# First SwiGLU's up projection with seven quarter products for eight, sums of its weights formed in two chains of DMAs

## The chip, the cores and the metric

The kernel runs on one core of a Trainium2 chip. The time is device microseconds of that core for one execution; lower is better. All data are float32.

## The reference

The reference is two transformer blocks over 512 tokens of width 1024. The first block has a Fourier mixer, a gated recurrence and a feed-forward layer with a depthwise convolution. The second block has two layers: retention and a SwiGLU, then a short convolution and another SwiGLU. Every layer is modulated by six vectors (shift, scale, gate, twice) that come from a product of a condition vector with the adaptive weights `ada_w`. Cut to what matters here:

```python
def swiglu(h, w1, w3, w2):
    return (jax.nn.silu(h @ w1) * (h @ w3)) @ w2

for i in range(2):
    sh1, sc1, g1, sh2, sc2, g2 = ada_params(c, ada_w[i], ada_b[i])
    ax = rms_norm(hx, norm_mix[i]) * (1 + sc1) + sh1
    hx = hx + g1 * (retention_mixer(ax, ...) if i == 0 else conv_mixer(ax, ...))
    fx = rms_norm(hx, norm_ffn[i]) * (1 + sc2) + sh2
    hx = hx + g2 * swiglu(fx, ffn_w1[i], ffn_w3[i], ffn_w2[i])
```

Here h is 512 x 1024, w1 and w3 are 1024 x 2816 and w2 is 2816 x 1024.

## The kernel before, in words

**Layout and stream of weights.** Activations lie transposed, channels on partitions and 512 tokens in the free dimension. All weights come as one stream of 377 blocks of 128 x 1024 floats (512 KB). SP loads a block into one of two raw buffers (`w_raw`); ScalarE rounds it to `w_hi` (`split_hi`, L435, the copy is L444), and VectorE forms `w_lo` as the rest (`split_lo`, L446, L452). There are four buffers of each, so the split of a block waits for the end of the block four back, and beside the work on block b the split of block b+3 is made. Each product is three matmuls: hi x hi, hi x lo, lo x hi (`three`, L487, its matmul is L493). SP loads block n when `lo_ready` shows that block n-2 is split. A block is 24 matmuls of 128x128 weights with 512 columns.

**Stages and block numbers.** Retention is blocks 122 to 185 (`B_RET`), four heads of 16 blocks. The first SwiGLU's up projection is blocks 186 to 229 (22 pairs of tiles, one of w1 and one of w3), its down projection 230 to 251 (`B_SD0`), the convolution's input 252 to 275 (`B_CIN`), its output 276 to 283, and the second SwiGLU's up projection starts at 284 (`B_SW1`). Between two stages stands a transition: the norm over channels is formed in two halves of 256 tokens, and the first tiles of the next stage run between (`transition_act`, L614; `transition_dve`, L676).

**The first SwiGLU** (`swiglu_pe` L1289, `swiglu_act` L1783, `swiglu_dve` L2310) is a loop over pairs of tiles: PE makes the w1 tile in a bank of `bx` and the w3 tile in a bank of `by`, ScalarE applies silu (L1799), VectorE multiplies, ScalarE and VectorE split the hidden tile into `hid_hi` and `hid_lo`. Beside each block ScalarE loads one row of adaptive weights (128 x 1024, `ada_load` L455) into one of two buffers `ada_raw`, and VectorE reduces it against the condition vector (`ada_reduce` L463; L474, then a short add L485). Rows 81 to 124 are loaded here; four rows are reduced in the down projection (`down_dve` L2388, `down_act` L1827), which updates the residual `res` after each of eight output tiles.

**The second SwiGLU** makes four pairs of tiles (`TILEWISE`) in the same way, and 18 pairs (`N_QUADS`) with seven quarter products for eight. For one pair the weights form a 2 x 2 matrix (w1 or w3, even or odd tiles of the contraction) and the activations too (even or odd tiles, first or second 256 tokens); seven products of four contraction tiles by 256 columns, of sums of weights and of activations, take the place of eight (`quad_pe` L980, matmul L1015). One pair takes 3.5 blocks of weights, 84 matmuls with 256 columns. VectorE forms four combinations of the activations beside the first four pairs (`sums_dve` L934, `combined_hi` L947, `combined_lo` L964), and VectorE and ScalarE put the products together (`quad_first_act` to `quad_hidden_lo`). Here four raw buffers are used, `w_raw` and `ada_raw`.

**The sums of weights** (W22+W11 and so on) are formed in DRAM by GpSimd's DMAs (L3036 to L3054), five for each pair, in one chain: two copies (`quad_first`, L3047), one adding transfer of 512 KB (`quad_more`, L3050), two adding transfers of 256 KB within `quad_sums` (L3052, L3054). Each waits for the one before it (`summed`) and for a block that paces it. There are 18 x 5 of them over 78 blocks from block 124. SP waits for all of them, and for all 128 reduced rows, before the first block of the seven-product part.

Of the kernel before, what the change touches and what calls it, by code (L numbers as in the profile page):

```python
# [18 lines left out]
F32 = mybir.dt.float32  # L19
# [5 lines left out]
P = 128  # L25
# [31 lines left out]
B_SD0 = B_SW0 + 2 * HT  # L57
# [3 lines left out]
TILEWISE = 4  # L61
N_QUADS = HT - TILEWISE
B_QUAD = B_SW1 + 2 * TILEWISE
B_SD1 = B_QUAD + 7 * N_QUADS // 2
# [12 lines left out]


# [76 lines left out]
def program(nc, wstream, quad_first, quad_more, quad_sums, ada_kn, ada_nk, x_in, ctx1_in, ctx2_in, cols_in, crow_in, ident_in, masks_in,  # L155
            dft1_in, dft2_in, rope_in, dec_in, out):
    with ExitStack() as ctx:
# [26 lines left out]
        quad_raw = w_raw + ada_raw  # L184
# [34 lines left out]
        for n, at in ((1, r_arena + 72 * KB), (2, r_hx + 16 * KB)):  # L219
# [59 lines left out]
                for s in range(2)]  # L279
# [3 lines left out]
        t_norm = sb("t_norm", [P, KT, L], F32, r_hc + 52 * KB)  # L283
        t_raw = sb("t_raw", [P, 4, KT // 2, L // 2], F32, r_hc + 68 * KB)
        t_at = [(r_hc + 88 * KB, r_hc + 92 * KB), (r_crow, r_crow + 4 * KB), None, (r_crow + 8 * KB, r_scr + 8 * KB)]
        t_hi, t_lo = ([None if at is None else sb(f"t{n}_{h}", [P, KT // 2, L // 2], F32R, at[h == "lo"])
                       for n, at in enumerate(t_at)] for h in ("hi", "lo"))
# [107 lines left out]
        summed = sem("summed")  # L395
# [31 lines left out]
        def raw_at(b):  # L427

            if b.at < B_QUAD:
                return w_raw[b.at % RAW], raw_ready[b.at % RAW], b.loads()  # L430
            n, s = divmod(b.at - B_QUAD, 4)
            return (quad_raw[s], *((raw_ready[s], 16 * (B_QUAD // RAW + n + 1)) if s < RAW else
                                   (ada_in[s - RAW], 16 * (128 // 2 + n + 1))))
# [29 lines left out]
        def ada_reduce(dve, a, row, i=None, per=0, row_c=None):  # L463

            landed = 16 * (a // 2 + 1)
            dve.wait_ge(ada_in[a % 2], landed if i is None else i * (16 * per // 2) + landed)
            n = a if i is None else i * per + a
            w = ada_raw[a % 2]
# [142 lines left out]
        def normalised(nm, j):  # L611
            return t_norm[:, j, :] if nm is nffn1 else tnorm[j % 2][:]
# [217 lines left out]
        COMBINED = [0, 1, 3, 2]  # L830
# [6 lines left out]
        JX["cin"] = JX["sw0"] + HT  # L837
# [4 lines left out]
        JY["sd0"] = JY["sw0"] + HT  # L842
# [68 lines left out]

        def place(g, n):

            return divmod(7 * g + n, 2)

        def made(engine, g, form):

            b, second = place(g, PRODUCTS[g % 2].index(form))
            if second:
                engine.wait_ge(block_done, B_QUAD + b + 1)  # L920
            else:
                engine.wait_ge(q_form, OPENED + b + 1)
# [5 lines left out]
        def combined(n, lo=False):  # L928

            if t_hi[n] is None:  # L930
# [2268 lines left out]
```

## Time and profile before

| | us |
|---|---|
| median of 3 runs (2257.71 to 2259.14) | 2259.04 |
| the profiled execution's own time | 2258.87 |
| its span | 2257.1 |
| PE busy | 2239.3 |
| DVE busy | 1483.9 |
| ACT busy | 868.9 |
| POOL busy | 232.3 |

PE is TensorE's matmuls, PEld its weight loads, DVE is VectorE, ACT ScalarE, POOL GpSimd, SP SyncE; a q behind a name is that engine's queue of DMA issues. Busy times overlap. A matmul's own duration in the trace overlaps with the next one's, so its price is the distance of two starts. A wait row says who waited, for whom, how long in total, how often and how long at most. Times in a view are counted from the start of the span. The 326 MB that the DMA engines move are 144 GB/s in the mean.

### The profile page before, as it was taken

What the parts mean: (1) busy time and instruction counts of PE and PEld (TensorE: products, weight loads), DVE (VectorE), ACT (ScalarE), POOL (GpSimd) and SP (SyncE); (2) the same over time, 40 slices, a digit from 0 to 9 for tenths busy, and PEclk for the clock granted to TensorE, in tenths of its full rate; (3) what the DMA queues carried; (4) which work ended last, traced back from release to release, by engine and by line L of the source; (5) the groups of instructions that cost most, each with busy time, mean ns of one, the idle gap of its engine ahead of it and who ended that gap; (6) DMA issues with size and microseconds to landing.
All of it is one profiled execution on the core that took longest, in us unless ns stands there. A gap on an engine that the chain in (4) does not pass through costs nothing.

```text
span 2257.1 us, 31951 instructions
## 1 busy us (share of the span) xinstructions
PE 2239.3 (99%) x11632; PEld 1906.4 (84%) x11632; DVE 1483.9 (66%) x2287; ACT 868.9 (38%) x1248; POOL 232.3 (10%) x187
## 2 busy tenths in 40 slices
PE   9999999999999999999999999999999999999998
PEld 4888888888888898888888878888889889999987
DVE  5558766689999866755746467665436446777622
ACT  4534442355554343313233244323224223554422
POOL 0000000036674001011110100100000000000000
PEclk9999999999999999999999999999999999999999
DMA  8442115423324628475765657876432332555421
GB/s 316 159 131 74 58 61 186 149 66 103 101 93 148 221 71 236 116 191 146 181 170 139 177 132 221 254 232 195 149 103 72 106 101 68 177 183 182 159 94 56
DMA packets 90939, 326.10 MB, mean 144 GB/s; under 512 B 10064, under 2 KB 10960, under 8 KB 89680
## 3 DMA queue, kind: packets, MB, share of 16 engines
q1 hardware_dynamic: 58432, 213.90, 28.5%
q10 hardware_dynamic: 19440, 72.96, 9.9%
q0 software_dynamic: 12960, 37.75, 8.4%
q8 instruction: 74, 1.21, 0.2%
q14 instruction: 33, 0.27, 0.0%
HBM read 322.48 MB, written 39.85 MB: 161 GB/s over the span
## 4 chain that ended last, share of the span: by engine, by line
PE 94%; DVE 3%; issue 1%; DMA 1%; ACT 1%; SPq 0%; DVEq 0%
PE bank L493 81%; PE bank L1015 8%; PE bank L1490 1%; DMA res<-in_x 1%; DVE rstd L680 1%; DVE hx_lo L692 0%; PE bank L1572 0%; PE bank L1348 0%; DMA w_raw<-in_wstream 0%; PE bank L1545 0%; DVE w_lo L452 0%; ACT hx_hi L627 0%; DVE tnorm L686 0%; PE bank L1514 0%; ACT w_hi L444 0%
## 5 line engine op out<-in xcount | busy, mean ns | idle before, releaser
L493 PE MATMUL bank<-hx_hi,w_hi 128*128 128x512 f32 (+1 forms) x1648 | 622.1, 377 | 5.3 <-DVE hx_lo L692 4.6
L493 PE MATMUL bank<-hx_hi,w_lo 128*128 128x512 f32 (+1 forms) x1648 | 611.6, 371 | 0.0
L493 PE MATMUL bank<-hx_lo,w_hi 128*128 128x512 f32 (+1 forms) x1648 | 611.6, 371 | 0.0
L452 DVE TENSOR_TENSOR w_lo<-w_raw,w_hi 128x1024 fp32r<-128x1024 f32 x290 | 354.7, 1224 | 343.5 <-ACT w_hi L444 339.7
L444 ACT ACTIVATE w_hi<-w_raw 128x1024 fp32r<-128x1024 f32 x335 | 353.8, 1056 | 426.5 <-PE bank L493 305.6
L493 PEld LDWEIGHTS bank<-hx_hi,w_hi 128*128 128x128 f32 x1648 | 311.2, 189 | 61.7 <-issue 4.9
L493 PEld LDWEIGHTS bank<-hx_hi,w_lo 128*128 128x128 f32 x1648 | 311.1, 189 | 53.2
L493 PEld LDWEIGHTS bank<-hx_lo,w_hi 128*128 128x128 f32 x1648 | 311.3, 189 | 52.8 <-issue 1.4
L2681 DVE SCALAR_TENSOR_TENSOR bank<-zpad,cols,bank 128x512 f32<-128x512 f32 x352 | 232.1, 773 | 4.6 <-ACT bank L2081 4.6
L493 PE MATMUL bank<-hid_hi,w_hi 128*128 128x512 f32 (+1 forms) x594 | 218.5, 368 | 0.0
L493 PE MATMUL bank<-hid_hi,w_lo 128*128 128x512 f32 (+1 forms) x594 | 217.2, 366 | 0.0
L493 PE MATMUL bank<-hid_lo,w_hi 128*128 128x512 f32 (+1 forms) x594 | 217.1, 366 | 0.0
L474 DVE CUSTOM_DVE_ANT_0 ada_raw<-ada_raw,crow 128x1024 f32<-128x1024 f32 x128 | 157.2, 1228 | 1.2 <-DMA ada_raw<-in_ada_nk 1.0
L493 PEld LDWEIGHTS bank<-hid_hi,w_lo 128*128 128x128 f32 x594 | 112.0, 189 | 18.2
L493 PEld LDWEIGHTS bank<-hid_hi,w_hi 128*128 128x128 f32 x594 | 112.0, 189 | 18.1
L493 PEld LDWEIGHTS bank<-hid_lo,w_hi 128*128 128x128 f32 x594 | 112.1, 189 | 17.8
L3005 POOL TENSOR_TENSOR w_lo<-w_raw,w_hi 128x1024 fp32r<-128x1024 f32 x44 | 105.2, 2408 | 5.6 <-ACT w_hi L444 5.5
L452 DVE TENSOR_TENSOR w_lo<-ada_raw,w_hi 128x1024 fp32r<-128x1024 f32 x42 | 51.5, 1225 | 53.9 <-ACT w_hi L444 53.9
L1015 PE MATMUL bank<-hx_hi,w_hi 128*128 128x256 f32 x288 | 81.6, 283 | 0.0
L1015 PE MATMUL bank<-hx_lo,w_hi 128*128 128x256 f32 x288 | 81.5, 283 | 0.0
L1015 PE MATMUL bank<-hx_hi,w_lo 128*128 128x256 f32 x288 | 81.5, 283 | 0.0
L444 ACT ACTIVATE w_hi<-ada_raw 128x1024 fp32r<-128x1024 f32 x42 | 44.5, 1060 | 67.3 <-PE bank L1015 43.9
(368 smaller groups left out, 3595.7 us busy)
## 6 DMA issues: line engine op xcount, KB each, us to landing
w_raw<-in_wstream SPq DMA_DIRECT2D x316, 512.0 KB, 3.5
ada_raw<-in_ada_nk ACTq DMA_DIRECT2D x128, 512.0 KB, 4.3
quad_sums<-in_quad_first POOLq DMA_DIRECT2D x36, 512.0 KB, 5.2
ada_raw<-in_wstream SPq DMA_DIRECT2D x25, 512.0 KB, 3.4
w_raw<-quad_sums SPq DMA_DIRECT2D x19, 512.0 KB, 3.8
quad_sums<-in_quad_more POOLq DMA_DIRECT2D x18, 512.0 KB, 7.6
quad_sums<-quad_sums POOLq DMA_DIRECT2D x36, 256.0 KB, 5.6
ada_raw<-quad_sums SPq DMA_DIRECT2D x17, 512.0 KB, 4.0
```

The source lines that it names most:

```text
L444: nc.scalar.activation(w_hi[nb.at % RING][:], src[:], ACT.Copy).then_inc(hi_ready, 1)
L452: nc.vector.tensor_tensor(w_lo[nb.at % RING][:], raw_at(nb)[0][:], w_hi[nb.at % RING][:].bitcast(F32), ALU.subtract).then_inc(lo_ready, 1)
L474: nc.vector.tensor_tensor_reduce(w[:], w[:], crow[:, row, :], 1.0, 0.0, ALU.mult, ALU.add, ada_sum[:, a % 4:a % 4 + 1]).then_inc(ada_done, 1)
L493: ins = nc.tensor.matmul(out_ap, s, m, start=first and at == 0, stop=last and at == n - 1)
L680: nc.vector.reciprocal(nm.rstd[:, HALF[h]], nm.std[:, HALF[h]]).then_inc(nm.rec, 1)
L1015: ins = nc.tensor.matmul(dst[:, HALF[half]], w[:, cut], mx, start=opens and j == 0 and m == 0, stop=j == KT // 2 - 1 and m == 2, skip_grou ...
L1490: ins = nc.tensor.matmul(dst, level_k[c % 2][:, h * P:(h + 1) * P], pair_halves(hq, c, r - 1, h), start=True, stop=True)
L2681: nc.vector.scalar_tensor_tensor(out=grid, in0=zpad[s][k][:, t // 3:t // 3 + ROWS, t % 3:t % 3 + GRID], scalar=cols[:, bass.ds(cw, 1)], in ...
L3005: nc.gpsimd.tensor_tensor(w_lo[nb.at % RING][:], w_raw[nb.at % RAW][:], w_hi[nb.at % RING][:].bitcast(F32), ALU.subtract).then_inc(lo_read ...
```

## The change

The first SwiGLU's up projection gets the form that the second has: four pairs tile by tile, 18 pairs with seven products. All functions of the form take the index w of the SwiGLU (0 or 1), and their code is used for both. With it:

- The stream is numbered anew: the first seven-product part is blocks 194 to 256, `B_SD0` is 257, `B_CIN` 279, `B_SW1` 311, the second seven-product part starts at 319, and there are 404 blocks. What SP loads and where to stands in a table (`loads`); SP's loop ends before block 194, and the rest of its list is written out.
- 36 pairs of weights need sums. Two chains run side by side, taken in turn: 24 pairs over blocks 124 to 180, 12 pairs over blocks 258 to 303.
- Rows 81 to 127 of the adaptive weights move: the reduction of row 80 stands in the first four pairs, rows 81 to 111 beside the first down projection, rows 112 to 127 beside the convolution's input, two to each group of three blocks. They use four buffers, `ada_raw` and two in the region of `crow`.
- The normalised activations of the first SwiGLU stay in a buffer of their own (`t_norm[0]`).

```diff
@@ constants
+QUAD_BLOCKS = 7 * N_QUADS // 2
+B_QUAD = [B_SW0 + 2 * TILEWISE]
+B_SD0 = B_QUAD[0] + QUAD_BLOCKS
...
+ADA_BEFORE = 81
+EARLY_SUMS = 24
...
@@ buffers
-        t_norm = sb("t_norm", [P, KT, L], F32, r_hc + 52 * KB)
+        t_norm = [sb(f"t_norm{w}", [P, KT, L], F32, r_hc + (16, 52)[w] * KB) for w in range(2)]
...
+        ada_more = [sb(f"ada_raw{s}", [P, D], F32, r_crow + 4 * KB * (s - 1)) for s in (2, 3)]
...
@@ loads
+        for n in range(N_BLOCKS):
+            for w in range(2):
+                if B_QUAD[w] <= n < (B_SD0, N_BLOCKS)[w]:
+                    loads[n] = landing(("raw0", "raw1", "ada0", "ada1")[(n - B_QUAD[w]) % 4], n)
+            if n not in loads:
+                loads[n] = landing("raw%d" % ((n if n < B_SD0 else n - B_SD0) % 2), n)
+            if n == B_SD0:
+                row_loads = {a: landing(("ada1", "ada0", "ada2", "ada3")[(a - ADA_BEFORE) % 4], None) for a in range(ADA_BEFORE, 128)}
...
@@ ada_load
+            if i is None and a >= ADA_BEFORE:
+                if a >= ADA_BEFORE + 4:
+                    act.wait_ge(ada_done, a - 3)
+                act.dma_start(row_loads[a][0][:], ada_nk[a]).then_inc(row_loads[a][1], 16)
+                return
...
@@ where rows and sums stand
-        SUMS = 5 * N_QUADS
-        SUMS_FROM, SUMS_OVER = B_RET + 2, (B_SW1 - B_RET - 6) // 2
+        ADA_ROWS = [range(ADA_BEFORE + (3 * n) // 2, ADA_BEFORE + (3 * n + 3) // 2) for n in range(HT - 1)]
+        CIN_ROWS = [range(112 + 2 * u, 114 + 2 * u) for u in range(KT)]
+        SUMS_IN = [(0, EARLY_SUMS, B_RET + 2, B_SW0 - 6), (EARLY_SUMS, 2 * N_QUADS, B_SD0 + 1, B_SW1 - 8)]
...
@@ SP
+            for w in range(2):
+                plain = B_QUAD[w] - w * 2 * N_QUADS
+                sp.wait_ge(ada_done, (ADA_BEFORE, 128)[w])
+                for c in range(2):
+                    sp.wait_ge(summed[c], 16 * 5 * (w + 1) * N_QUADS // 2)
+                for n in range(B_QUAD[w], (B_QUAD[1], N_BLOCKS)[w]):
+                    slot, landed, _, previous = loads[n]
+                    if previous is not None:
+                        sp.wait_ge(lo_ready, previous + 1)
...
+                    sp.dma_start(slot[:], src).then_inc(landed, 16)
...
@@ PE
-            swiglu_pe(pe, B_SW0, JX["sw0"], JY["sw0"], nffn0)
-            hidden_down_pe(pe, B_SD0, JY["sd0"], sw_l[0], 0, nmix1, none)
+            def quads_pe(w):
+                for g in range(N_QUADS):
+                    quad_pe(pe, w, g)
+                pe.wait_ge(q_post, OPENED + 4 * (N_QUADS * w + N_QUADS - 1))
...
+            swiglu_pe(pe, B_SW0, JX["sw0"], JY["sw0"], nffn0, TILEWISE)
+            quads_pe(0)
+            hidden_down_pe(pe, B_SD0, JY["sd0"], sw_l[0], 0, nmix1, lambda ct: quads_out(0) if ct == 0 else None)
...
@@ ScalarE
-            swiglu_act(act, 0, B_SW0, JX["sw0"], JY["sw0"], 80)
-            down_act(act, B_SD0, JY["sd0"], [(nmix1, None)], lambda n: ada_load(act, 125 + n) if n < 3 else None, none)
...
+            quads_act(0)
+
+            def rows_act(n):
+                if n == 0:
+                    act.wait_ge(block_done, B_SD0)
+                    act.wait_ge(lo_ready, B_SD0)
+                for a in [*(ADA_ROWS[0] if n == 0 else ()), *(ADA_ROWS[n + 1] if n + 1 < len(ADA_ROWS) else CIN_ROWS[0])]:
+                    ada_load(act, a)
+
+            down_act(act, B_SD0, JY["sd0"], [(nmix1, None)], rows_act, none)
...
@@ ScalarE, in the convolution's input, after the second tile of a group
+                    for a in (CIN_ROWS[4 * i + u + 1] if 4 * i + u + 1 < KT else ()):
+                        ada_load(act, a)
...
@@ VectorE
-            swiglu_dve(dve, 0, B_SW0, JY["sw0"], 80)
-            modulation(88, COLS["mix"] + 8, 8)
-            down_dve(dve, B_SD0, JY["sd0"], lambda j: ada[:, 72 + j:73 + j], (nmix1,),
-                     lambda n: ada_reduce(dve, 124 + n, ROW_C2) if n < 4 else None)
-            dve.wait_ge(ada_cols, 128)
+            quads_dve(0)
+
+            def rows_dve(n):
+                for a in (ADA_ROWS[n] if n < len(ADA_ROWS) else ()):
+                    ada_reduce(dve, a, ROW_C2)
+                if n < len(ADA_ROWS) and 95 in ADA_ROWS[n]:
+                    dve.wait_ge(ada_cols, 96)
+                    modulation(88, COLS["mix"] + 8, 8)
+
+            down_dve(dve, B_SD0, JY["sd0"], lambda j: ada[:, 72 + j:73 + j], (nmix1,), rows_dve)
+            dve.wait_ge(ada_cols, 112)
...
@@ VectorE, in the convolution's input, after each of the first two splits of a group
+                        if kind < 2:
+                            ada_reduce(dve, CIN_ROWS[4 * i + u][kind], ROW_C2)
...
@@ GpSimd
+            def summing(first, last, since, until):
+                for q in range(first, last, 2):
+                    for step in range(5):
+                        for c in range(2):
+                            at = 10 * ((q - first) // 2) + 2 * step + c
+                            pool.wait_ge(block_done, since + at * (until - since) // (5 * (last - first)))
+                            if q or step:
+                                pool.wait_ge(summed[c], 16 * (5 * (q // 2) + step))
...
+            for part in SUMS_IN:
+                summing(*part)
```

## Rows read from the trace of the kernel before

**Rows 1.** The page: its span, and the first line of its part 1.
```profile
span 2257.1 us, 31951 instructions
...
PE 2239.3 (99%) x11632; PEld 1906.4 (84%) x11632; DVE 1483.9 (66%) x2287; ACT 868.9 (38%) x1248; POOL 232.3 (10%) x187
```

**Rows 2.** Chain that ended last, 1943 to 2125 us: start us, us, what.
```profile
1943.03 5.75 PE bank L1015 x48
1948.77 0.04 issue
1948.81 175.91 PE bank L1015 x1464
```

**Rows 3.** Timeline of ACT, 1562 to 1592 us: start us, us, engine, line, operation.
```profile
1563.60 1.04 ACT L444 ACTIVATE w_hi<-w_raw 128x1024 fp32r<-128x1024 f32 x1
...
1574.48 1.04 ACT L444 ACTIVATE w_hi<-w_raw 128x1024 fp32r<-128x1024 f32 x1
```

**Rows 4.** Busy by stage: length, PE, PEld, DVE, ACT, POOL, clock, DMA, GB/s.
```profile
824.00:970.00 146.00, 146.00 (x767) 125.29 (x768) 110.85 (x168) 54.50 (x84) 12.80 (x18) 1.00 0.58 160
1358.00:1480.00 122.00, 122.00 (x613) 104.23 (x613) 82.89 (x133) 41.09 (x56) 10.71 (x15) 1.00 0.80 244
1600.00:1700.00 100.00, 100.00 (x445) 82.90 (x444) 33.40 (x38) 23.27 (x25) 0.00 (x0) 1.00 0.35 110
...
1943.00:2125.00 182.00, 181.96 (x1515) 181.73 (x1514) 136.00 (x191) 92.57 (x138) 0.00 (x0) 1.00 0.56 184
```

**Rows 5.** DMA queues and issues, 1358 to 1480 us; last: us to landing.
```profile
q10 hardware_dynamic: 3306, 12.05, 29.3%
q1 hardware_dynamic: 3260, 11.85, 28.2%
q0 software_dynamic: 2044, 5.82, 22.5%
...
quad_sums<-in_quad_first POOLq DMA_DIRECT2D x6, 512.0 KB, 6.3
quad_sums<-quad_sums POOLq DMA_DIRECT2D x6, 256.0 KB, 7.4
quad_sums<-in_quad_more POOLq DMA_DIRECT2D x3, 512.0 KB, 9.3
```

**Rows 6.** Timeline of POOL, the first eleven issues of sums.
```profile
845.51 0.70 POOL L3047 DMA_DIRECT2D quad_sums<-in_quad_first  x1 [127.89 <-PE bank L493]
...
911.33 0.54 POOL L3047 DMA_DIRECT2D quad_sums<-in_quad_first  x1 [5.55 <-DMA quad_sums<-quad_sums]
```

**Rows 7.** Instructions of L474 on DVE, 1358 to 1620 us.
```profile
L474 DVE CUSTOM_DVE_ANT_0 ada_raw<-ada_raw,crow x48: 1217/1219/1226, 1370.1 to 1613.4; 128x1024 f32<-128x1024 f32 x48
L474 DVE DVE_READ_ACCUMULATOR2_ANT ada_sum<- x48: 81/83/88, 1371.3 to 1614.5; 128x1 f32 x48
```

**Rows 8.** Timeline of ACT, 1386 to 1392 us.
```profile
1390.23 1.06 ACT L444 ACTIVATE w_hi<-w_raw 128x1024 fp32r<-128x1024 f32 x1 [0.86 <-DMA w_raw<-in_wstream]
```

**Rows 9.** Waits of PE: who waited for whom, us in total, times, longest us.
```profile
PE bank L493 <- DVE res L2722: 1.7, 5, 0.6
```

**Rows 10.** Instructions of L1146, all: duration ns, first and last start us.
```profile
L1146 SPq DMA_DIRECT2D w_raw<-in_wstream x24: 327/332/338, 1926.1 to 2205.3; - x24
```

**Rows 11.** Waits of DVE, 1358 to 1620 us.
```profile
DVE ada_raw L474 <- DMA ada_raw<-in_ada_nk: 0.7, 1, 0.7
```

**Rows 12.** Chain that ended last, 1320 to 1340 us.
```profile
1325.34 7.74 DMA w_raw<-in_wstream
...
1336.22 3.91 PE bank L493 x16
```

**Rows 13.** Busy time, clock and DMA share of three short windows.
```profile
1348.00:1351.00 3.00, 0.56 (x5) 0.35 (x3) 2.71 (x4) 1.49 (x3) 0.53 (x1) 1.00 0.44 123
1351.00:1354.00 3.00, 2.78 (x16) 2.52 (x17) 2.96 (x7) 0.56 (x2) 0.83 (x1) 0.76 0.16 60
1354.00:1358.00 4.00, 4.00 (x25) 3.94 (x25) 3.89 (x10) 3.50 (x7) 0.00 (x0) 0.75 0.94 174
```

More of the change, by code:

```diff
@@ L394, in program, with landing @@
         t_sum, t_hi_ready, t_lo_ready, t_shifted = opened[6:10]
-        summed = sem("summed")
+        ada_in_more = opened[10:12]
+        summed = [sem(f"summed{c}") for c in range(2)]
+        loads = {}
+        counts = {"ada0": (ADA_BEFORE + 1) // 2, "ada1": ADA_BEFORE // 2, "ada2": 1, "ada3": 1}
+        slots = {"raw0": (w_raw[0], raw_ready[0]), "raw1": (w_raw[1], raw_ready[1]), "ada0": (ada_raw[0], ada_in[0]),
+                 "ada1": (ada_raw[1], ada_in[1]), "ada2": (ada_more[0], ada_in_more[0]), "ada3": (ada_more[1], ada_in_more[1])}
+        last_in = {}
+        def landing(name, n):
+            counts[name] = counts.get(name, 0) + 1
+            before_it, last_in[name] = last_in.get(name), n
+            return (*slots[name], 16 * counts[name], before_it)
+        for n in range(N_BLOCKS):
[6 more added lines that the diff above has]
+                row_loads = {a: landing(("ada1", "ada0", "ada2", "ada3")[(a - ADA_BEFORE) % 4], None) for a in range(ADA_BEFORE, 128)}
         class Norm:
@@ L1013, in quad_pe @@
                     xh, xl = x(j)
-                    for m, (w, mx) in enumerate(((w_hi[slot], xh), (w_hi[slot], xl), (w_lo[slot], xh))):
-                        ins = nc.tensor.matmul(dst[:, HALF[half]], w[:, cut], mx, start=opens and j == 0 and m == 0,
+                    for m, (form_w, mx) in enumerate(((w_hi[slot], xh), (w_hi[slot], xl), (w_lo[slot], xh))):
+                        ins = nc.tensor.matmul(dst[:, HALF[half]], form_w[:, cut], mx, start=opens and j == 0 and m == 0,
                                                stop=j == KT // 2 - 1 and m == 2, skip_group_check=True)
@@ L1127, in _ @@
                 crow_load(row, crow_landed)
-            with sp.Fori(1, B_QUAD // RAW - 1) as i:
+            with sp.Fori(1, B_QUAD[0] // RAW - 1) as i:
                 for s in range(RAW):
@@ L2904, in _, with quads_dve, combinations @@
             dve.wait_ge(nffn0.lo, nffn0.tiles + 2 * KT)
[L2905 to L2909 removed]
+            def quads_dve(w):
+                made_sums = sums_dve(dve, w)
+                def combinations(u):
+                    if w == 0 and u == 0:
+                        ada_reduce(dve, ADA_BEFORE - 1, ROW_C2)
+                    if 1 <= u < 4:
+                        next(made_sums)
+                        if u == 2:
+                            next(made_sums)
+                            combined_lo(dve, w, 0, 1)
+                        elif u == 3:
+                            combined_lo(dve, w, 1, 2)
+                            combined_lo(dve, w, 3, 3)
+                swiglu_dve(dve, w, (B_SW0, B_SW1)[w], JY["sw0" if w == 0 else "sw1"], None, TILEWISE, combinations)
+                for u in range(TILEWISE, 4):
+                    combinations(u)
+                for g in range(N_QUADS):
+                    at = list(windows(g))
+                    split_lo(dve, Block(B_QUAD[w] + at[0]))
+                    if g == 0:
+                        combined_lo(dve, w, 2, 4)
+                    else:
+                        quad_hidden_dve(dve, w, g - 1)
+                    split_lo(dve, Block(B_QUAD[w] + at[1]))
+                    if g >= 1:
+                        quad_hidden_lo(dve, w, g - 1)
+                    quad_mid_dve(dve, w, g)
+                    split_lo(dve, Block(B_QUAD[w] + at[2]))
+                    quad_inner_dve(dve, w, g)
+                    for b in at[3:]:
+                        split_lo(dve, Block(B_QUAD[w] + b))
+                    quad_outer_dve(dve, w, g)
+                quad_hidden_dve(dve, w, N_QUADS - 1)
+                quad_hidden_lo(dve, w, N_QUADS - 1)
```

339 lines of the change are left out of this document (154 added, 185 removed).

## The prediction

> **What bounds the kernel now.** I read the page first: PE is busy for 2239.3 of 2257.1 us [rows 1]. PE is the bound in nearly every stage, so a change counts by the PE time it removes and by the waits it puts in front of PE. Second the chain that ended last, over the second SwiGLU, where the seven-product form runs already: 48 and 1464 matmuls of 256 columns from 1943.03 to 2124.72 (1948.81 plus 175.91), with 0.04 us of issue between them [rows 2]. This is the price of what the first SwiGLU is to get. Third ScalarE's timeline in the first SwiGLU, for the price of what goes: a split of a block starts when the block four before it is done, so equal splits are one tile pair apart [rows 3]. Fourth the busy time by stage [rows 4], because the change moves transfers and VectorE work between stages. Fifth the DMA queues where weights, adaptive rows and sums already run together [rows 5], and the sums' own pace on GpSimd [rows 6].
>
> **The products.** A pair of tiles of the first SwiGLU takes 10.88 us (1574.48 less 1563.60) [rows 3]: 48 matmuls of 512 columns, 226.7 ns each. A pair by seven products is 84 matmuls of 256 columns; 18 pairs take 181.69 us together, 10.09 us a pair, 120.2 ns a matmul [rows 2]. Half the columns cost more than half the time (113.3 ns), so an eighth less work gives 7.2%. Eighteen pairs: 18 x 10.88 = 195.8 us go, 181.7 come: **-14.1 us**.
>
> The Trainium skill (TensorE: Matmul & The Clock Gate, Back-to-back issue gap) gives an isolated gap of N/2.4 + 2.5 ns, so 215.8 and 109.2 ns. By that the sum would be 18 x (48 x 0.2158 - 84 x 0.1092) = 21.3 us saved, an estimate. The trace measures 226.7 and 120.2 ns for these very forms, so the measured 14.1 stays.
>
> **The work around them.** Forming the four combinations of activations, the opening of the banks and the last wait before the down projection are copies of what the second SwiGLU does. There DVE is busy for 136 of 182 us, ACT for 92.6, and PE for 181.96 of 182 [rows 4]; what hides them is PE's own time. VectorE has one thing more in the opening four tiles, the reduction of row 80 (1.22 us and some 0.3 us of small instructions) [rows 7]; in the first SwiGLU before, VectorE makes such a reduction beside every block, and PE still has 122.00 of 122 us [rows 4]. If that cover were gone it would cost 1.5 us once. I take 0.
>
> **SP's queue.** From block 194 on SP runs an unrolled list. It first waits for 81 reduced rows and for 45 transfers of each chain of sums; behind that wait stand all later weight loads. The row is reduced at the start of the SwiGLU, before SP could issue this load anyway, whose buffer comes free later. For the second SwiGLU it waits for row 128 (reduced in the convolution) and the last sums. In time both cost 0; late, they are rival 2.
>
> **Sums in retention.** Before, one chain makes 18 tiles, paced over 78 blocks; afterwards two chains make 24 tiles over 56 blocks. GpSimd issues them and has nothing else there. An unpaced step takes 6.6 us (845.51 to 911.33, ten steps) [rows 6]. The plan: 64 blocks run between 824 and 1358 us [rows 4], 8.3 us each, so 60 steps of a chain in 467 us, 7.8 us a step. GpSimd takes the chains in turn, so both go at the pace of the slower. No row shows two chains. Below: 6.6 us a step, as alone. Above: 13.2, one chain's transfer wholly behind the other's. I take 9.5, nearer the first, since only a part of a step is transfer: three tiles of five steps take 22.5% of 122 us, 9.2 us a tile, 1.8 a step [rows 5]. The first 18 tiles then need 45 x 9.5 = 428 us and are ready at 1273, well before 1390.23, when block 194 was split before [rows 8]. The last six run on to 845 + 570 = 1415, beside the first products, whose share of DMA is 0.56 [rows 4]; two chains add 2 x 9.2/47.5 = 0.39. That fits. In retention they raise 0.58 [rows 4] by 0.39 less 9.2/33 = 0.28, to 0.7. Weight blocks land somewhat later, but are split two to three blocks ahead. I take 0; bounds -0.6 (the longest wait for res there goes) [rows 9] and +6 (rival 3).
>
> **Rows and sums beside the first down projection.** Rows 81 to 124 leave the SwiGLU. 31 rows (81 to 111) are loaded and reduced beside 21 of the 22 down blocks, where four were before, and 16 beside the convolution's input. VectorE per block of 5.44 us (24 of 226.7 ns): a split 1.2, 1.5 rows at 1.5, updates and squares 0.5, together 4.0 us; before it was busy for 33.4 of 100 us [rows 4, 7]. It fits. ScalarE only issues. For DMA I use the 122 us with all three kinds [rows 5]: 28.2% for 23 blocks is 1.50 us a block, 29.3% for 23 rows 1.55 us a row, and 9.2 us a tile of sums. In the down stage: blocks 1.50/5.44 = 0.28, rows 31 x 1.55/119.7 = 0.40, sums as planned 12 x 9.2/(45 x 5.44) = 0.45. Together **1.13, more than there is**. So something is late. If it is the sums, planned from 1600 over 245 us and needed about 1926, when SP issued the first loads of the second seven-product part before [rows 10], it costs nothing. If it is the rows, VectorE falls behind by up to 0.13 x 119.7 = 15.6 us by the end, of which 7 are covered, since the last row is due at step 20 of 22: +8. I take 0, because rows are issued a block ahead into four buffers, and at share 0.80 [rows 4] VectorE waited 0.7 us for rows in all [rows 11]. In the convolution: blocks 0.28, rows 16 x 1.55/131 = 0.19, sums 0.45: 0.92, which fits; its first reduction goes ahead of a split that waits for ScalarE anyway.
>
> **Sum.** Profiled execution 2258.87 us (span 2257.1 and 1.8 around it), 0.2 us below the median of the three runs, 2259.04. 2258.87 - 14.1 = **2244.8 us**. A measurement of this kernel can tell 0.2% (4.5 us) from no change.
>
> **Rivals.**
> 1. *The rows are what waits* in the overfull down stage, and VectorE is late for the transition. For it: 1.13, and two chains at once. Against: PE 122.00 of 122 at 0.80. Price up to +8: 2245 to 2253, say 2250. The Trainium skill (DMA: Bandwidth & Descriptors, Queues, rings and completion order) says that each engine goes round the queue rows packet by packet; both chains are on GpSimd's one queue, so by it the sums can't crowd out the other two, and the shortage falls on them. No row here shows a full stage.
> 2. *The chains of sums are too slow and SP stands still.* Place: SP's two waits. Block 194's load must go by about 1388, so 45 steps have 543 us: it decides from 12.1 us a step. The last 12 tiles, 30 steps, have from 1600 to about 1933: 11.1 us. Each us a step beyond costs 45 or 30 us, so from 11.6 us in the second part the gain is gone (0.5 x 30 = 15). At 13.2 both are late, by 594 - 543 = 51 and 396 - 333 = 63 us: 2359 us, **slower**. For it: with one chain under load the landings have medians of 6.3, 9.3 and 7.4 us [rows 5], 7.3 a step and with the issue above 8. Against: they would have to grow by half again.
> 3. *Weight blocks land late in retention.* The load at 1325.34 took 7.74 us with a sum in flight, and PE's matmul at 1336.22 hung on its split [rows 12]. If two chains make that 9.3, as the slowest kind of sum [rows 5], it is +1.6 at each of four heads: 2251. Against: the chain of waits shows this at one head only, and there PE was kept 0.6 us at most [rows 9].
> 4. *The clock.* PE was busy for only 0.56 of the 3 us from 1348; the granted clock was then 0.76 and 0.75 for 7 us, so for some 3.5 us at the level of 1.2 GHz: 0.24 x 3 + 0.25 x 4 = 1.7 us lost [rows 13]. If that goes, 2243.1.
>
> **How the numbers follow.** Forecast 0.70; rival 1 0.12, rival 2 0.04, rival 3 0.09, rival 4 0.05. Low end 2258.87 - 14.1 - 1.7 - 0.6 = 2242.5. High end 2251, with rival 3 and most of rival 1. Left out are rival 2 and the top of rival 1, together under 0.1. Faster by over 0.2% means below 2254.5: all but rival 2 and 0.02 for rivals 1 and 3 coming together: 0.94. Same 0.02, slower 0.04.
>
> **What would show it.** The first SwiGLU's 1512 seven-product matmuls take about 182 us with PE busy throughout, and no new wait stands before them. DMA share above 0.9 in the first down projection, the sums landing 8 us and more after issue and ending late; VectorE waiting for rows by some us, PE for none. ScalarE's waits for weights grow in retention without PE's. Wrong would be: PE waiting for w_lo at block 194 or in the second SwiGLU (rival 2), for res or w_lo in the down projection (rival 1), or a matmul spacing other than 120 ns.

## The result, and the profile after

| | before | after |
|---|---|---|
| median of 18 runs each, us | 2258.31 (2257.38 to 2259.63) | 2266.97 (2261.3 to 2276.02) |
| ratio | | 1.0039, 95% interval 1.0032 to 1.0046 |
| profiled execution's own time, us | 2258.87 | 2264.04 |

The change makes the kernel slower by 0.4%, where the prediction had it faster by 0.6%. The runs of after are also far more spread: 15 us from the fastest to the slowest, against 2.

I read the page first. Its lines for span, PE and the chain that ended last:

```profile
span 2262.2 us, 32938 instructions
...
PE 2230.9 (99%) x12280; PEld 1928.4 (85%) x12280; DVE 1559.0 (69%) x2419; ACT 908.5 (40%) x1321; POOL 295.2 (13%) x277
...
PE bank L530 60%; PE bank L1057 16%; DMA w_raw<-in_wstream 8%; DVE w_lo L480 2%; ACT w_hi L472 1%; PE bank L1536 1%; DMA ada_raw<-in_ada_nk 1%; DVE hx_lo L729 1%; DMA res<-in_x 1%; DVE rstd L717 1%; PE bank L1618 0%; PE bank L1394 0%; DVE cacc L3044 0%; PE bank L1591 0%; DVE rstd L2911 0%
```

PE is busy for 8.4 us less than before [rows 1], yet the span is longer. So PE now waits, and the chain says for what: DMA's loads of `w_raw` alone hold 8% of it, 180 us.

Next PE's waits (engine, line of the matmul, line of what it waited for: total, times, longest):

```profile
PE bank L530 <- DVE cy_lo L3052: 8.2, 1, 8.2
PE bank L530 <- DVE res L2786: 4.6, 5, 3.3
...
PE bank L530 <- DVE w_lo L480: 3.2, 6, 1.9
```

New are one wait of 8.2 us for `cy_lo` (the convolution's input), one of 3.3 us for `res` in retention, where the longest was 0.6 before [rows 9], and longer waits for splits (`w_lo`). Third the busy time by stage, with the granted clock, DMA's share and GB/s last in each line: retention, the seven-product part, the down projection, transition and convolution's input, then five short stretches around the two long waits.

```profile
845.00:1313.00 468.00, 464.03 (x2127) 385.58 (x2126) 281.19 (x402) 142.21 (x199) 84.92 (x120) 0.99 0.85 214
1404.00:1586.00 182.00, 181.96 (x1515) 181.75 (x1514) 135.76 (x190) 92.55 (x138) 0.00 (x0) 1.00 0.57 178
1586.00:1705.00 119.00, 118.71 (x574) 100.06 (x574) 79.22 (x136) 29.83 (x35) 17.09 (x25) 1.00 1.01 329
1727.00:1850.00 123.00, 119.87 (x526) 97.78 (x525) 75.18 (x113) 34.40 (x45) 21.18 (x30) 1.00 0.92 255
1103.00:1106.00 3.00, 0.59 (x1) 0.50 (x2) 2.62 (x4) 1.79 (x3) 1.28 (x2) 0.77 0.75 92
1106.00:1109.00 3.00, 3.00 (x9) 2.32 (x8) 1.75 (x3) 0.00 (x0) 0.76 (x1) 0.50 0.77 200
1109.00:1113.00 4.00, 4.00 (x14) 3.21 (x13) 0.75 (x1) 0.00 (x0) 0.62 (x2) 0.70 0.96 248
1855.00:1859.00 4.00, 0.00 (x0) 0.00 (x0) 3.09 (x6) 1.11 (x2) 0.00 (x0) 0.57 0.43 131
1859.00:1863.00 4.00, 3.64 (x10) 2.94 (x11) 3.16 (x5) 2.04 (x3) 0.00 (x0) 0.58 0.29 69
```

The seven-product part is as forecast: 181.96 us of PE in 182, as in the second SwiGLU [rows 4]. The down projection, with DMA full (1.01), costs PE 0.3 us. The losses are in the two stretches where DMA's share is 0.85 and 0.92. And after each long wait PE runs slower for a while: after PE had been busy for 0.59 of 3 us the granted clock was 0.50 of full speed (that is 1.2 GHz) with PE busy throughout the next 3 us, and after the wait for `cy_lo` (0.00 us of 4) it was 0.57 and 0.58 for two stretches of 4 us. At the first that is 3 x 0.46 + 3 + 4 x 0.6 = 6.8 us at the lower level, at the second 4 x 0.86 + 4 x 0.84 = 6.8 us; in the first PE still stood for some 0.8 us of the 6.8, so it costs some 3.0 us, and in the second for more than half, so it costs some 1.5.

What delays the transfers shows in the median time from issue to landing, here for the weight blocks in the transition and the convolution's input, where the copies of the sums took 7.8:

```profile
w_raw<-in_wstream SPq DMA_DIRECT2D x22, 512.0 KB, 8.2
```

The chain around the wait for `cy_lo` (start, us, what) shows how a late block reaches PE:

```profile
1809.34 8.59 DMA w_raw<-in_wstream
...
1817.94 1.07 ACT w_hi L472
...
1820.18 0.69 DVE cpad L3035
...
1824.26 1.05 ACT w_hi L472
...
1825.33 1.24 DVE w_lo L480
...
1826.59 10.74 DMA w_raw<-in_wstream
...
1845.99 6.10 DMA w_raw<-in_wstream
...
1852.12 1.06 ACT w_hi L472
...
1854.35 0.69 DVE cpad L3035
...
1857.88 0.64 ACT cy_hi L2341
...
1859.36 2.93 PE bank L530 x6
```

The chain returns to a load once in three blocks: 1809.34, 1826.59, 1845.99. In between stand the landing and 8.66 us of work that is made one after the other: ScalarE's `w_hi`, the multiply and the steps of `cacc` on VectorE (`cpad` to `cacc` L3048, 3.5 us), `cy_hi`, the next `w_hi`, the next `w_lo`, and only then does SP load into the raw buffer that this frees. PE's work in three blocks is 72 matmuls of 226.7 ns, 16.3 us. By this working the stage stands landings of 16.3 - 8.66 = 7.7 us, an estimate from one chain; at 8.59 and 10.74 us the turns took 17.25 and 19.40. Single later ones it stands as long as blocks are split ahead: of the 14.5 us lost behind block 190 (the table below) some 12 fell in the last group of the convolution. At the end VectorE, in order, waits for `w_hi` (1852.12) of a block that PE needs only later, with the `cacc` steps that PE needs now behind it.

The same in retention, once in this run:

```profile
1092.34 9.82 DMA w_raw<-in_wstream
...
1102.26 1.06 ACT w_hi L472
...
1103.35 0.05 DVE w_lo L480
...
1104.61 0.76 DVE res L2786
```

A load took 9.82 us; VectorE stood before the split of that block, and behind it the update of `res` that frees PE's bank.

### The profile page after: what moved, and what is told of

It reads as the page before. It is cut to its first block, busy times and chain, and to the rows that moved or that the text cites. A ratio compares the mean times of both kernels' runs of the same rounds, so it can differ in the third digit from the quotient of the medians.

```text
span 2262.2 us, 32938 instructions
## 1 busy us (share of the span) xinstructions
PE 2230.9 (99%) x12280; PEld 1928.4 (85%) x12280; DVE 1559.0 (69%) x2419; ACT 908.5 (40%) x1321; POOL 295.2 (13%) x277
## 4 chain that ended last, share of the span: by engine, by line
PE 80%; DMA 9%; DVE 6%; ACT 2%; issue 2%; SPq 0%; DVEq 0%; ACTq 0%
PE bank L530 60%; PE bank L1057 16%; DMA w_raw<-in_wstream 8%; DVE w_lo L480 2%; ACT w_hi L472 1%; PE bank L1536 1%; DMA ada_raw<-in_ada_nk 1%; DVE hx_lo L729 1%; DMA res<-in_x 1%; DVE rstd L717 1%; PE bank L1618 0%; PE bank L1394 0%; DVE cacc L3044 0%; PE bank L1591 0%; DVE rstd L2911 0%
## 5 line engine op out<-in xcount | busy, mean ns | idle before, releaser
L530 PE MATMUL bank<-hx_hi,w_hi 128*128 128x512 f32 (+1 forms) x1360 | 510.2, 375 | 7.4 <-DVE hx_lo L729 4.2
L530 PE MATMUL bank<-hx_lo,w_hi 128*128 128x512 f32 (+1 forms) x1360 | 499.7, 367 | 0.0
L530 PE MATMUL bank<-hx_hi,w_lo 128*128 128x512 f32 (+1 forms) x1360 | 499.6, 367 | 0.0
L530 PEld LDWEIGHTS bank<-hx_hi,w_hi 128*128 128x128 f32 x1360 | 257.2, 189 | 53.6 <-issue 7.8
L530 PEld LDWEIGHTS bank<-hx_hi,w_lo 128*128 128x128 f32 x1360 | 257.1, 189 | 42.4
L530 PEld LDWEIGHTS bank<-hx_lo,w_hi 128*128 128x128 f32 x1360 | 257.4, 189 | 41.0 <-issue 1.4
L1057 PE MATMUL bank<-hx_hi,w_hi 128*128 128x256 f32 x576 | 163.1, 283 | 0.1
L1057 PE MATMUL bank<-hx_hi,w_lo 128*128 128x256 f32 x576 | 163.0, 283 | 0.0
L1057 PE MATMUL bank<-hx_lo,w_hi 128*128 128x256 f32 x576 | 163.0, 283 | 0.0
L1057 PE MATMUL bank<-t_hi,w_hi 128*128 128x256 f32 x432 | 122.3, 283 | 0.0
```

What stands on the lines that cost most here:

```text
L530: ins = nc.tensor.matmul(out_ap, s, m, start=first and at == 0, stop=last and at == n - 1)
L1057: ins = nc.tensor.matmul(dst[:, HALF[half]], form_w[:, cut], mx, start=opens and j == 0 and m == 0, stop=j == KT // 2 - 1 and m == 2, skip ...
```

## The experiments

Eleven kernels ran. For a common measure the table gives, for one profiled execution of each, how much later the last matmul of a block ended than in the run without sums, with the difference at block 110 taken off (worked out from the traces' matmuls). So each column is a loss made in one stretch of one execution, and the medians need not follow it. The medians are over the runs of each.

| run | until block 120 | retention, to 190 | down projection to convolution's input, to 306 | median us |
|---|---|---|---|---|
| after | 0.0 | 6.1 | 14.5 | 2266.97 |
| e1_no_sums | 0 | 0 | 0 | 2244.24 |
| e2_no_late_sums | 0.0 | 9.7 | 0.0 | 2250.75 |
| e3_no_early_sums | 0.0 | -0.1 | 20.2 | 2259.84 |
| e4_no_row_loads | 0.0 | 0.3 | 0.0 | 2245.2 |
| e5_order | 0.0 | 0.0 | 13.3 | 2259.5 |
| f1_four_raw | 0.0 | 3.4 | 0.6 | 2246.36 |
| f2_sums_from_102 | 15.6 | 3.8 | 18.0 | 2280.4 |
| f3_all | 17.1 | 9.6 | 0.3 | 2265.05 |
| f5_all_30 | 13.7 | 3.2 | 0.0 | 2263.16 |
| g1_four_raw_res_first | 0.0 | 0.0 | 0.6 | 2243.63 |
| g2_all_orders | 0.0 | 0.2 | 0.0 | 2243.96 |

**e1_no_sums.** Are the sums the whole loss?

```diff
-                for c in range(2):
-                    sp.wait_ge(summed[c], 16 * 5 * (w + 1) * N_QUADS // 2)
...
-                        src = quad_sums[w * N_QUADS + 2 * q + half // 4, :, (half - 1) % 3 * BLK:((half - 1) % 3 + 1) * BLK]
+                        src = quad_first[w * N_QUADS + 2 * q + half // 4, :, (half - 1) % 3 * BLK:((half - 1) % 3 + 1) * BLK]
...
-            for part in SUMS_IN:
-                summing(*part)
```

> The changed kernel without any of the sums' transfers: SP reads the unsummed quad_first in place of quad_sums (same bytes, same pace) and waits for no sum. Left out: the sums of weights. Contention theory (the sums' transfers make weight blocks land late, the two raw buffers then pace PE, in-order VectorE is late): all the loss of 20 us goes, 2243 to 2247 us, spread of a few tenths as in the kernel before. Rival (the new form, the moved reductions on VectorE or SP's new waits cost it): 2260 us or more. Mixed: in between.

Measured: 2244.24 us (2243.88 to 2244.89), ratio 0.9938 (0.9925 to 0.995). That is the forecast of 2244.8 to 0.6 us, with the same products, rows and splits. All of the 22.7 us that after loses against it comes with the sums. The busy time of the transition and the convolution's input (the columns as above):

```profile
1727.00:1850.00 123.00, 122.69 (x541) 101.27 (x541) 80.99 (x118) 37.92 (x48) 0.00 (x0) 1.00 0.48 156
```

And the landing of its blocks in that stretch:

```profile
w_raw<-in_wstream SPq DMA_DIRECT2D x25, 512.0 KB, 3.6
```

PE works 122.69 of 123 us, DMA's share is 0.48, a block lands in 3.6 us.

**e2_no_late_sums** (the last 12 tiles are not formed) and **e3_no_early_sums** (the first 24 are not): do the two losses add?

```diff
-            for part in SUMS_IN:
+            for part in SUMS_IN[:1]:
```

```diff
-            for part in SUMS_IN:
+            for part in SUMS_IN[1:]:
```

> Only the second part of the sums is left out (12 tiles over blocks 258 to 303); the last 12 pairs read unsummed weights. Contention theory: what the profile shows lost in the convolution's input and behind it (about 11 us and more in slower runs) goes, the 5.5 us of retention stay: 2249 to 2253 us, spread smaller. Rival (the early sums in retention are the main cost): above 2258 us.

> The first 24 tiles' sums are left out (those blocks are read from the first quarter's forms, so the second factor's sums are missing there); the last 12 tiles are made as in the changed kernel, with its two raw buffers. Theory (the losses of the two stretches are separate and add): the retention is as before, the convolution's input loses what it lost in the changed kernel (cy_lo wait of 4 to 8 us with its half clock, 12 to 14 us in all), so 2244.2 + 12 to 16 = 2256 to 2260. Rival (the convolution loses because the retention has put the stages out of step): under 2252.

Measured: 2250.75 us (2247.47 to 2253.19) and 2259.84 us (2255.33 to 2270.36). Over the run without sums that is 6.5 us for the early sums and 15.6 for the late ones, together 22.1 of 22.7. The loss of the late sums comes without the early ones and the other way round, so they are separate. That the two medians add to within 0.6 us is partly luck: e4_no_row_loads and f1_four_raw below have the retention of e2_no_late_sums and lose 1.0 and 2.1 us in all over the run without sums, where this one lost 6.5. PE's waits in e3_no_early_sums:

```profile
PE bank L530 <- DVE cy_lo L3052: 5.7, 1, 5.7
PE bank L530 <- DVE w_lo L480: 4.8, 8, 2.8
...
PE bank L575 <- DVE std L555: 2.2, 1, 2.2
PE bank L530 <- DVE res L2786: 1.4, 4, 0.6
```

The wait for `cy_lo` is there, and `res` is back at 0.6. The wait for `std`, the norm's sum of squares, is at the end of the down projection: VectorE made it behind the split of a block that took 9.35 us to land and behind the reduction of one row. With the half clock after it that is 4.2 of the 20.2 us of the table; in after the same place lost 0.8. In e2_no_late_sums it is the other way:

```profile
PE bank L530 <- DVE res L2786: 6.3, 4, 3.4
```

**e4_no_row_loads.** Rows 81 to 127 are not loaded; their reductions stay on VectorE, with the condition row for both factors. All sums stay.

```diff
-                act.dma_start(row_loads[a][0][:], ada_nk[a]).then_inc(row_loads[a][1], 16)
```

> Rows 81 to 127 are not loaded; their reductions stay on VectorE, of the condition row with itself. Left out: those rows of the adaptive weights. All sums stay. Theory that both kinds of transfer must come together to be too much: the down projection falls from a DMA share of 1.0 to 0.6 and the convolution's input from 0.92 to 0.75, loads land near 6 us, the loss behind 1586 us goes, 2249 to 2254 us. Rival (the sums alone are enough): 2260 us or more.

Measured: 2245.2 us (2244.19 to 2251.65), ratio 0.9951 (0.9939 to 0.9964), 4 us under the range that I expected, since the retention lost less than 5. With the sums in place and DMA's share still 0.82 a block lands in 6.1 us in the convolution's input:

```profile
w_raw<-in_wstream SPq DMA_DIRECT2D x24, 512.0 KB, 6.1
```

6.1 + 8.66 = 14.8 us is under the 16.3 of three blocks, and the stretch loses nothing. So the sums alone don't make the late loss: it needs landings as late as rows and sums make together. That the retention lost nothing in this profile is chance: its code and its transfers are those of after, and so are e5_order's, with 0.0.

**e5_order.** In the convolution's last group the split of the block three ahead goes behind the `cy` steps, on ScalarE and VectorE.

```diff
-                        if i or u or kind:
+                        if (i or u or kind) and 3 * (4 * i + u) + kind < 23:
                             split_lo(dve, Block(B_CIN + 3 * u + kind, i, 12))
...
+            split_lo(dve, Block(B_COUT - 1))
             dve.wait_ge(ada_cols, 128)
```

> Everything as in the changed kernel, but in the last of the eight groups of the convolution's input ScalarE and VectorE do the split of the block three ahead after the convolution's own chain (cacc, cy_hi, cy_lo) and not before it. Theory (in-order engines: the chain PE needs stands behind a split that waits for a late block; the wait then halves PE's clock): the 8.2 us wait for cy_lo and the 3.4 us of low clock behind it shrink to the 0.3 us of before, 2256 to 2261 us. Rival (the wait only moves, since the same late block is missing next): no change beyond 2 us from 2267.

Measured: 2259.5 us (2255.35 to 2266.34, and one run of 6035.72 us; without it the median is 2258.41), ratio 1.0009 (1.0 to 1.0018), 7.5 us under after. PE's waits:

```profile
PE bank L530 <- DVE w_lo L480: 5.0, 11, 1.9
...
PE bank L530 <- DVE cy_lo L3054: 3.6, 1, 3.6
```

The wait for `cy_lo` is 3.6 us instead of 8.2, but PE waits 5.0 us for splits, 11 times: the order doesn't cure the stretch, and the loop of load, splits and `cacc` before it stays too slow. How much the order itself brings isn't shown: in the profiled executions the stretch lost 13.3 us instead of 14.5, and the rest of the difference is the retention, which has the same code in both.

**f1_four_raw.** The mechanism's own test: leave all traffic, and give the loads more time.

```diff
+        raw_more = [sb(f"raw_more{s}", [P, BLK], F32, r_hc + (88 + 4 * s) * KB) for s in range(2)]
...
+            if B_SD0 + 4 <= n < B_SW1:
+                loads[n] = landing(("raw2", "raw3", "raw0", "raw1")[(n - B_SD0) % 4], n)
...
+                    if n == B_SD0 + 4:
+                        sp.wait_ge(block_done, B_SD0)
```

> From block 261 on (second half of the first SwiGLU's down stage, the transition, the convolution's input) the weight blocks have four raw buffers instead of two; nothing else differs from the changed kernel. Theory (what costs the time behind the first SwiGLU is the latency of the block loads: with two buffers a pair of blocks comes every landing time + 2.4 us, so 8.2 us of landing is too much for 10.9 us of products): the waits for cy_lo go back from 8.2 us to under 1 us, the half clock at their side goes, the splits' margins before the products stay over 5 us, and the time is 2266.97 - 10 = about 2257, at most 2260; the retention's loss of about 5 us stays. Rival (the DMA engines' throughput itself is what lacks in that stretch: 92% are busy): blocks then queue deeper and land later still, and the time stays at 2264 to 2268.

Measured: 2246.36 us (2244.96 to 2248.15), ratio 0.9948 (0.9935 to 0.9961). The stretch of the convolution's input:

```profile
1727.00:1850.00 123.00, 122.69 (x542) 101.27 (x541) 80.83 (x119) 36.58 (x46) 20.54 (x29) 1.00 0.96 266
```

The landings there, of the two old raw buffers and of the two new ones:

```profile
w_raw<-in_wstream SPq DMA_DIRECT2D x12, 512.0 KB, 7.0
raw_more<-in_wstream SPq DMA_DIRECT2D x12, 512.0 KB, 7.5
```

DMA's share is higher than in after (0.96), the blocks land in 7.0 to 7.5 us, and PE works 122.69 of 123 us, as without any sums. The rival, that throughput is short, falls: the stage lacked buffers, not bandwidth. These medians are under the 7.7 us, so this run alone doesn't show that four buffers stand later landings; f3_all does. It has four buffers too (and the order of e5_order), and loses nothing here with a median of 8.0 in `w_raw` (7.2 in the other two):

```profile
1754.00:1877.00 123.00, 122.69 (x542) 101.27 (x541) 79.22 (x115) 38.16 (x48) 20.30 (x28) 1.00 0.93 257
...
w_raw<-in_wstream SPq DMA_DIRECT2D x12, 512.0 KB, 8.0
```

Nor is the median landing the measure for two buffers. f2_sums_from_102, with two, has 7.3 us in the same stretch (both are later than after here, by what they lost before), and PE stands still for 4.9 of 123 us:

```profile
1746.00:1869.00 123.00, 118.13 (x512) 95.09 (x510) 71.33 (x106) 32.90 (x43) 20.02 (x28) 1.00 0.92 252
...
w_raw<-in_wstream SPq DMA_DIRECT2D x21, 512.0 KB, 7.3
```

Its longest landing there is 13.2 us, after's 11.6, that of e4_no_row_loads, which loses nothing, 7.9. So single late blocks count, and the 7.7 us of the mean turn is no limit below which nothing is lost.

The time of f1_four_raw came out 10 us lower than I expected. Of the 20.6 us under after, 15.6 is what e3_no_early_sums showed for the late sums (I had expected 10); the rest would be the retention, which lost less in these runs than in those of e2_no_late_sums (2.1 us over the run without sums, against 6.5), with the same code there. Why, stays open.

**f2_sums_from_102.** A lower rate of sums in retention, by an earlier start.

```diff
-        SUMS_IN = [(0, EARLY_SUMS, B_RET + 2, B_SW0 - 6), (EARLY_SUMS, 2 * N_QUADS, B_SD0 + 1, B_SW1 - 8)]
+        SUMS_IN = [(0, EARLY_SUMS, B_DOWN + 2, B_SW0 - 6), (EARLY_SUMS, 2 * N_QUADS, B_SD0 + 1, B_SW1 - 8)]
```

> The first 24 tiles' sums are spread over blocks 102 to 180 instead of 124 to 180, a step of a tile each 10 us or so instead of 7.8; the last 12 tiles as in the changed kernel. Theory (in the retention the sums' rate sets the share of the DMA engines, 0.85, and with it the landing of the blocks, 6.4 us): the share there falls to about 0.78, the blocks land in about 5.6 us, no load of nearly 10 us falls beside a res update, and the time falls by 3 to 6 us to 2261 to 2264. Rival (the loss is made by any single late load, however rare, or by the stretch before 124 having no room either): no change, or a new wait before block 124; 2266 to 2270.

Measured: 2280.4 us (2277.31 to 2281.62), ratio 1.0095 (1.0081 to 1.011), worse than both. DMA's share from 845 to 1313 fell to 0.72, but the stretch before it, the last transition before retention, suffers. Its busy time, the granted clock third from the end:

```profile
770.00:800.00 30.00, 25.72 (x105) 20.82 (x104) 21.73 (x41) 10.45 (x17) 5.27 (x7) 0.89 0.94 253
800.00:845.00 45.00, 41.15 (x249) 36.49 (x248) 27.26 (x45) 17.21 (x27) 8.32 (x13) 0.92 0.90 216
```

The chain there (start, us, what):

```profile
767.26 9.30 DMA w_raw<-in_wstream
...
779.07 10.56 DMA w_raw<-in_wstream
...
790.62 0.70 ACT sq L546
...
792.49 0.44 DVE c_std L555
```

Loads took 9.30 and 10.56 us there, and the sums of squares and the `std` of the norm, which PE waits for (4.3 us for `c_std` and 3.5 for `std`, with the clock at 0.89 and 0.92), stood behind the splits. Neither of my numbers held; the rival named the place. The 3.8 us of its second column fall before block 150, next to this transition; from there to block 190 this execution lost nothing.

**f3_all** (four raw buffers, the early start, the order of e5_order) and **f5_all_30** (the same with 30 tiles early and 6 late):

```diff
-EARLY_SUMS = 24
+EARLY_SUMS = 30
```

> Both of the above (four raw buffers from block 261 on, the first 24 tiles' sums spread from block 102 on) and the order in the convolution's last group (the split of the block that is three ahead stands behind the last cy operations on ScalarE and VectorE). Theory: all of what the sums cost but the down stage's 0.9 us is back: 2245 to 2250, faster than before by 0.4 to 0.6%. Rival (throughput): the order alone brings what it did, 2257 to 2262.

> As the run of all three edits, with 30 of the 36 tiles of sums made early (blocks 102 to 180) and 6 late instead of 24 and 12. The first part's rate is then again about that of the changed kernel (a step each 8 us), the second's is halved. Theory (retention's loss comes from the rate): the retention loses its 5 us again and the late stages nothing, 2249 to 2253, slower than with 24 and 12. Rival (the late stages still lose more than the retention): 2244 to 2248, faster than with 24 and 12.

Measured: 2265.05 us (2261.88 to 2272.44) and 2263.16 us (2260.64 to 2265.29). Both miss, since both hold the early start, which costs 17.1 and 13.7 us before block 120. What they do show: behind the first SwiGLU both lose at most 0.3 us, and in f3_all some 6 of the 9.6 us of the second column were lost in the middle of retention (one wait of 4.0 us for `res`, and the half clock), although the rate of sums was lower and DMA's share only 0.72. So the loss there doesn't go by the rate alone.

**g1_four_raw_res_first** and **g2_all_orders.** If in retention it is the split ahead of the update that makes the loss, the order cures it at the full rate. The second adds the order of e5_order.

```diff
             def wo_dve(b0, jy, i, head0, split_from=0, nm=None, beside=none):
...
-                    if n >= split_from:
-                        split_lo(dve, b)
                     for u in range(2):
...
+                    if n >= split_from:
+                        split_lo(dve, b)
                     beside(n)
```

> As the run with four raw buffers, and in the retention's output projections VectorE makes both updates of the residual (which free TensorE's banks) before the split of the block three ahead, not behind it. Theory (the retention loses by a late load that holds VectorE ahead of an update): no wait for res over 1 us, no half clock in the retention, 2244 to 2245.5, 1 to 2 us under the run with four raw buffers alone (2246.4). Rival (the late loads hit the products themselves, or the later split makes the next load late): 2246 to 2250, with waits for w_lo in the retention.

> As the run before (four raw buffers, updates of the residual first), and the order of the convolution's last group (split behind the last cy operations). Theory: the buffers already cover the convolution's input, so the order adds at most the 0.6 us that stretch still loses: 2243.5 to 2245.5. Rival (the order costs once the buffers are there): over 2246.

Measured: 2243.63 us (2243.14 to 2245.74) and 2243.96 us (2243.44 to 2245.35), both with a ratio of 0.9938 (0.9925 to 0.9951). The first one's PE waits:

```profile
PE bank L535 <- DVE w_lo L485: 0.6, 4, 0.2
PE bank L535 <- DVE res L2791: 0.6, 1, 0.6
```

Its busy time in retention, and in the transition with the convolution's input:

```profile
845.00:1313.00 468.00, 467.57 (x2151) 388.36 (x2150) 285.50 (x403) 146.76 (x204) 84.83 (x120) 1.00 0.87 216
1727.00:1850.00 123.00, 122.69 (x541) 101.28 (x540) 79.36 (x115) 38.16 (x48) 20.06 (x28) 1.00 0.93 259
```

DMA's share is 0.87 and 0.93, as high as in after, a block in retention still lands in 6.6 us (6.4 in after), and PE works as without sums. Against f1_four_raw, the kernel that it differs from by the order alone, this is 2.7 us less. The ranges of two sets of five runs overlap there, but over g1 and g2 together the longest of ten runs is 2245.74, and over the three kernels that have the old order and no late loss (e2_no_late_sums, e4_no_row_loads, f1_four_raw) the fifteen runs go up to 2253.19. So the order takes the retention's losses away. The whole loss is gone, with every sum and row in place, and this version beats both kernels: faster than the kernel before by 0.6%. The order in the convolution adds nothing once the buffers are there.

## Why the prediction was wrong

**The products, -14.1 us: right.** The seven-product part took PE 181.96 us of 182, and the run without sums came to 2244.24 us against the forecast 2244.8. By the gap that the Trainium skill gives (TensorE: Matmul & The Clock Gate, Back-to-back issue gap) it would have been 2258.87 - 21.3 = 2237.6, an estimate; the measured spacing was the better price.

**The work around them, SP's queue: right.** No wait stood before the seven-product part, and SP waited for no sum. Rival 2 did not occur: the 60 steps of a chain began at 845.2 and the last at 1298.3 us, 7.7 us a step, the planned pace. I had taken 9.5; two chains hardly delayed each other. The share was mis-sized by this: I had 0.7 in retention, and it was 0.85. Two chains at 7.7 us a step take 0.54, with 10.5 us of all engines a tile (53.6% of 468 us for 24 tiles) where I had 9.2. And my 0.58 was from a stretch whose first 21 us had no sums; from 845 to 1313 it was 0.62 before.

**Rows and sums in the down projection: nearly right in the outcome.** The share was full, 1.01 at 329 GB/s, as the sum of 1.13 said. The shortage fell on the sums: rows took 39.9% and blocks 26.7%, as in my sum, and the sums 34.2% where 45 were planned. VectorE waited 17.2 us for rows in 15 waits, and PE lost 0.8 us against the run without sums. So rival 1 did not occur in after. In a small form it did in e3_no_early_sums: VectorE was late for the norm, for 4.2 us. The Trainium skill (DMA: Bandwidth & Descriptors, Queues, rings and completion order) says that each engine goes round the queue rows packet by packet; I had concluded that the sums can't crowd out the others. For throughput the trace agrees, with the shares above. The time to landing it did not protect: blocks landed in 7.9 us instead of 4.4 in the run without sums, and in the convolution's input in 8.2 instead of 3.6.

**The first step that failed: "In the convolution: blocks 0.28, rows 0.19, sums 0.45: 0.92, which fits".** The share was right, 0.92, and it was the wrong measure. What decided is whether blocks land as soon as the loop through two buffers needs them. A turn needs a block's landing plus 8.66 us in the 16.3 us of three blocks, which leaves 7.7; the landing was 8.2 in the median and up to 11.6. Put at 0, the late sums cost 15.6 us in the median (e3_no_early_sums; in its profiled execution 4.2 of it at the end of the down projection). With four buffers and the same traffic it was 0.6 or less (f1_four_raw, g1_four_raw_res_first, g2_all_orders). The down projection, fuller still, has 10.88 us for two blocks and only the two splits (1.06 + 1.24 us) in its loop, which leaves some 8.5 us for a landing of 7.9 (its median there). That would explain why the fuller stage lost so little until its last blocks; it was read from the trace, and no run tested it by itself. I had worked out what each engine has to do in a stage, and not the loop through two engines and a buffer.

**The second: "Weight blocks land somewhat later, but are split two to three blocks ahead. I take 0", in retention.** It cost 6.5 us in the median of e2_no_late_sums and at most 2.1 and 1.0 in those of f1_four_raw and e4_no_row_loads, which have the same code there; in the profiled execution of after it was 6.1, with a landing of 6.4 us instead of 4.9 and single ones of up to 9.8. The distance of two to three blocks is PE's cover against a late split. It doesn't cover what stands behind the late split on VectorE, and there stood the update of `res` that PE was waiting for. g1_four_raw_res_first moved that update ahead, and the loss was gone. Rival 3 had the right event, a late load in retention. It had the victim wrong (the split itself, where it was the update behind it), and the price of one event too low, 1.6 us where it was 3.3 and some 3.0 for the half clock; that its 6.4 us for four heads is near the largest of the medians is luck.

**The range.** My upper bound for retention, +6, holds two of the three medians and is just short of the third, 6.5 us; for the convolution I had no bound at all, because "it fits" had closed the question. My 0.04 for slower stood for the stopped SP alone.

**The clock.** Rival 4's price per dip was right in kind: PE idle for some 3 us, then 3.4 or 6.8 us at half pace. I counted only a dip that might go, and none that might come. The dip that I priced stayed in after (a clock of 0.53 from 1357 to 1360 us).

## What to carry to other kernels

A share of DMA time below 1 doesn't say that a transfer is hidden. Measure the landing at that share, and compare it with what the loop of load, split and release leaves per turn; two buffers with 8.66 us of other work in the loop left 7.7 us, and lost time with medians of 7.3 to 8.2; four lost at most 0.6 us with medians of up to 8.0. Look at the longest landings too, not only at the median. On an engine that works in order, put what TensorE waits for next ahead of any work that may wait for a transfer, and count what is behind each wait. Before moving traffic into an earlier stage, look for its norms and transitions: the start at block 102 cost 15 us where the retention could have won 6 at most.

## What the runs showed of the hardware

- In the transition and the convolution's input the median landing of a 512 KB block was 3.6 us at a share of 0.48 (no sums), 6.1 at 0.82 (no rows), 8.2 at 0.92 (both), and 7.0 to 7.5 at 0.96 (both, with four buffers); single loads took up to 11.6 us in after and 13.2 in f2_sums_from_102.
- The same retention code, with the same transfers, lost between 0.0 and 9.7 us in five profiled executions (0.0, 0.3, 3.4, 6.1, 9.7); in after it was one load of 9.82 us. The runs of after scatter by 15 us, those of the kernel before by 2.
- A wait of PE doesn't always cost clock. After 3.3 us of waiting (PE busy for 0.59 of 3 us) the granted clock was half for 6.8 us. In f1_four_raw PE waited up to 2.8 us for `res`, and its clock stayed at 1.00. PE's waits for `res`:

```profile
PE bank L535 <- DVE res L2793: 5.2, 4, 2.8
```

The stretch with the longest of them:

```profile
1100.00:1125.00 25.00, 22.23 (x98) 18.10 (x97) 14.23 (x20) 6.26 (x7) 4.56 (x7) 1.00 0.88 231
```
